# Seven block products in place of eight for the gate and up projections of two pairs of chunks per gated feed-forward

## The chip, the core and the metric

The kernel runs on one core of a Trainium2 chip. TensorE multiplies matrices from SBUF into PSUM, VectorE and ScalarE work on rows and evict PSUM, GpSimd does small things, and SyncE's queue issues the weight loads. The metric is the device time of one execution in microseconds. The kernel before takes 1432.91 us (median of 3 runs, 1431.85 to 1433.77).

## What is computed

The input is one sequence of 256 rows of 1024. A first block (adaptive norm, two kinds of attention, a convolutional feed-forward) is followed by a second block of two layers, each with a gated feed-forward, a mixer, and another gated feed-forward. The change concerns these four feed-forwards:

```python
D_FF = 2816

def swiglu(h, wg, wu, wd):
    return (jax.nn.silu(h @ wg) * (h @ wu)) @ wd

# second_block, for l in (0, 1):
    h = rmsnorm(x, g[0])
    x = x + 0.5 * rmsnorm(swiglu(h, ffn_wg[l, 0], ffn_wu[l, 0], ffn_wd[l, 0]), g[1])
    ...
    h = rmsnorm(x, g[4])
    x = x + 0.5 * rmsnorm(swiglu(h, ffn_wg[l, 1], ffn_wu[l, 1], ffn_wd[l, 1]), g[5])
```

All data are float32.

## The kernel before

**Split products.** Each float32 factor is split into a high part (rounded to the format that TensorE multiplies at full rate, fp32r) and a low part (the rest). A product is three matmuls: high by high, high by low, low by high (line 2552 to 2554). ScalarE writes the high part of a weight tile from the loaded raw tile in two activations of 128x1024 (`split_hi`, line 1936), VectorE the low part in two subtractions (`split_lo`, line 2147).

**Tiles.** A *unit* is a weight tile of 128x2048 floats, 1 MB. Three raw buffers (`RAW`) take the loads in order; SyncE issues a load when the tile three loads earlier has both its parts (line 1756). Three pairs of split buffers (`w_hi`, `w_lo`), and in the stretches of units named by `WIDE` two more (`hi_qk`, `hi_at` and their low ones, in memory that only the attentions use), take the parts. All four gated feed-forwards lie in wide stretches. A tile's split waits until the tile five units before it has been used (`plan.before`, `unit_used`).

**A gated feed-forward.** The columns of the gate and up matrices are cut into 11 chunks (`NFC`) of 256 (`FC`). A chunk has two units, for the input features 0 to 511 and 512 to 1023; each holds, per 128 features, 256 gate columns and 256 up columns. `chunk` (line 2556) runs for each of the 4 feature tiles of a unit and each of the 2 token tiles one split product: stationary the tokens (`hT_hi`, `hT_lo`, 128x128), moving the 512 weight columns, into one PSUM bank per token tile. ScalarE then applies silu to the gate half and VectorE multiplies it with the up half (`upout`, lines 2092 and 2463, one instruction per token tile), TensorE transposes the hidden rows (`hturn`, line 2797), ScalarE and VectorE evict them as `hc_hi` and `hc_lo` (lines 2100 and 2472), and the down projection (one unit, 24 matmuls) adds to four PSUM banks that live through the whole feed-forward.

**Order.** The order is written out by a planner: `build_plan` makes one list of steps, and each engine walks this list and emits its own part of each step, so within an engine's queue the steps stand in this order. `split_ahead(u)` (line 235) puts in, ahead of the product of unit u, the splits of all units up to u + 4 (with five buffers) that are not in yet. `FfnHead.go_on` (line 855) begins a feed-forward: products of chunks 0 and 1 for the second token tile, `upout`, `hturn(0)`, `down(0)`, `hturn(1)`, and then for each chunk from 2 to 9: products of its two units, `upout`, `down` of the chunk before, `hturn`. `tail` does chunk 10 and crosses into the next stage. The lines of `go_on` that matter:

```python
            self.mm(2, 1)
            self.hidden_turn(0)
            pl.split_to(us[3] + 2)
            self.mm(3, 1)
            self.out(1)
            ...
            self.down(0)
            self.hidden_turn(1)
```

`mm(i, t)` is the product of the i-th unit of chunks 0 and 1 with token tile t. `us[3] + 1` is the down unit of chunk 0, `us[3] + 2` the first unit of chunk 2. `down(0)` first calls `split_ahead` for its own unit, so three more units are split in the steps between `out(1)` and `hidden_turn(1)`.

## Time and profile before

| | |
|---|---|
| median of the runs | 1432.91 us |
| profiled execution | 1431.2 us of span |
| TensorE matmul, busy | 1392.6 us (97%), 7039 instructions |
| TensorE weight load, busy | 1157.8 us (81%) |
| VectorE, busy | 926.0 us (65%), 1401 |
| ScalarE, busy | 758.1 us (53%), 1249 |
| weight loads by SyncE | 250.87 MB |
| granted TensorE clock, mean | 0.993 |

Times are from one profiled execution. "Busy" counts instructions that run; matmuls overlap in the pipeline, so their number times their own duration is more than the time they take. A granted clock of 1 is 2.4 GHz, of 0.50 is 1.2 GHz. The four feed-forwards run, roughly, from 440 to 620, 758 to 940, 945 to 1130 and 1248 to 1430 us.

### The profile page before, as it was taken

The numbers are of one execution on the slowest core, as the hardware profiler recorded it, in microseconds if no ns is written. First come the engines' busy times: TensorE is split into PE (matmuls) and PEld (weight loads), VectorE is DVE, ScalarE is ACT, GpSimd is POOL, SyncE is SP. The second block draws the span as 40 slices with busy tenths as digits, with TensorE's granted clock in tenths as the row PEclk, the third lists the DMA queues.
The fourth block names the chain that finished last, engine by engine and source line by source line (L and its number), as shares of the span: only waits on it lengthen the run. The fifth ranks groups of instructions, "written<-read, shape, count | busy, mean of one in ns | idle before, by whom it ended". The sixth has DMA issues, their size and how long they took to land.

```text
span 1431.2 us, 19205 instructions
## 1 busy us (share of the span) xinstructions
PE 1392.6 (97%) x7039; PEld 1157.8 (81%) x7039; DVE 926.0 (65%) x1401; ACT 758.1 (53%) x1249; POOL 79.3 (6%) x133
## 2 busy tenths in 40 slices
PE   4999999999999999999899999999999999999998
PEld 4878877999988888887778888888888877788886
DVE  5677787799777554479986555476545556675453
ACT  4456746755456444366576444465444467574442
POOL 3011100000000000021300000000000100000000
PEclk9999999999999999999999999999999999999999
DMA  9887656477645765544355765547555373565550
GB/s 352 279 293 263 195 173 195 146 268 245 227 146 176 231 196 181 177 133 148 118 173 178 226 199 181 176 134 257 183 185 197 121 210 118 191 230 182 188 165 30
DMA packets 177596, 274.36 MB, mean 192 GB/s; under 512 B 6465, under 2 KB 120897, under 8 KB 177505
## 3 DMA queue, kind: packets, MB, share of 16 engines
q1 hardware_dynamic: 170800, 250.87, 53.2%
q0 software_dynamic: 5552, 20.20, 4.6%
q10 hardware_dynamic: 1153, 2.07, 0.4%
q8 instruction: 58, 0.95, 0.3%
q14 instruction: 33, 0.27, 0.1%
HBM read 272.05 MB, written 1.06 MB: 191 GB/s over the span
## 4 chain that ended last, share of the span: by engine, by line
PE 78%; DVE 4%; issue 1%; ACT 1%; POOL 0%; DVEq 0%; POOLq 0%; ACTq 0%
PE psum L2552 22%; PE psum L2554 22%; PE psum L2553 22%; PE psum L2595 2%; PE psum L2594 2%; PE psum L2592 2%; PE psum L2797 1%; DVE w_lo L2147 1%; PE psum L2649 1%; PE psum L2721 1%; PE psum L2750 0%; DVE attn L2324 0%; PE psum L2664 0%; DVE work L2301 0%; PE psum L2703 0%
## 5 line engine op out<-in xcount | busy, mean ns | idle before, releaser
L2147 DVE TENSOR_TENSOR w_lo<-raw,w_hi 128x1024 fp32r<-128x1024 f32 (+1 forms) x312 | 371.9, 1235 | 115.4 <-ACT w_hi L1936 114.5
L2552 PE MATMUL psum<-w_hi,hT_hi 128*128 128x512 f32 x888 | 357.3, 402 | 6.4 <-DVE hT_lo L2247 3.7
L1936 ACT ACTIVATE w_hi<-raw 128x1024 fp32r<-128x1024 f32 (+1 forms) x312 | 310.8, 1050 | 98.6 <-PE psum L2554 62.2
L2554 PE MATMUL psum<-w_hi,hT_lo 128*128 128x512 f32 x888 | 347.8, 392 | 0.0
L2553 PE MATMUL psum<-w_lo,hT_hi 128*128 128x512 f32 x888 | 347.3, 391 | 0.0
L2552 PEld LDWEIGHTS psum<-w_hi,hT_hi 128*128 128x128 f32 x888 | 167.8, 189 | 45.5 <-issue 10.2
L2554 PEld LDWEIGHTS psum<-w_hi,hT_lo 128*128 128x128 f32 x888 | 167.5, 189 | 36.5
L2553 PEld LDWEIGHTS psum<-w_lo,hT_hi 128*128 128x128 f32 x888 | 168.1, 189 | 32.8 <-issue 0.5
L2147 DVE TENSOR_TENSOR lo_qk<-raw,hi_qk 128x1024 fp32r<-128x1024 f32 (+1 forms) x72 | 84.1, 1209 | 32.5 <-ACT hi_qk L1936 31.8
L2552 PE MATMUL psum<-w_hi,hc_hi 128*128 128x512 f32 x256 | 100.3, 392 | 0.6 <-DVE hc_lo L2472 0.6
L2554 PE MATMUL psum<-w_hi,hc_lo 128*128 128x512 f32 x256 | 99.8, 390 | 0.0
L2553 PE MATMUL psum<-w_lo,hc_hi 128*128 128x512 f32 x256 | 99.7, 389 | 0.0
L2092 ACT ACTIVATE PR<-psum,stat 128x256 f32<-128x256 f32 x88 | 37.6, 472 | 116.0 <-PE psum L2554 114.8
L2147 DVE TENSOR_TENSOR lo_at<-raw,hi_at 128x1024 fp32r<-128x1024 f32 (+1 forms) x72 | 84.2, 1208 | 19.7 <-ACT hi_at L1936 19.4
L2463 DVE SCALAR_TENSOR_TENSOR PR<-psum,stat,PR 128x256 f32<-128x256 f32 x88 | 39.0, 480 | 88.9 <-ACT PR L2092 88.9
L1936 ACT ACTIVATE hi_qk<-raw 128x1024 fp32r<-128x1024 f32 (+1 forms) x72 | 71.4, 1042 | 36.4 <-PE psum L2554 25.1
L2100 ACT ACTIVATE hc_hi<-psum 128x512 fp32r<-128x512 f32 (+1 forms) x48 | 26.9, 561 | 113.1 <-PE psum L2797 113.1
L2472 DVE TENSOR_TENSOR hc_lo<-psum,hc_hi 128x512 fp32r<-128x512 f32 (+1 forms) x48 | 31.0, 646 | 85.1 <-ACT hc_hi L2100 85.1
L1936 ACT ACTIVATE hi_at<-raw 128x1024 fp32r<-128x1024 f32 (+1 forms) x72 | 71.4, 1042 | 25.7 <-PE psum L2554 15.6
L1880 POOL TENSOR_TENSOR stat<-stat,minus_half 128x1 f32<-128x1 f32 (+2 forms) x24 | 17.2, 715 | 1140.8 <-DVE stat L2230 1062.9
L2552 PE MATMUL psum<-hi_qk,hT_hi 128*128 128x512 f32 (+1 forms) x176 | 69.0, 392 | 0.0
L2554 PE MATMUL psum<-hi_qk,hT_lo 128*128 128x512 f32 (+1 forms) x176 | 67.9, 386 | 0.0
(236 smaller groups left out, 2335.5 us busy)
## 6 DMA issues: line engine op xcount, KB each, us to landing
raw<-in_ffn_wg_dram SPq DMA_DIRECT2D x88, 512.0 KB, 4.0
raw<-in_ffn_wu_dram SPq DMA_DIRECT2D x88, 512.0 KB, 5.0
raw<-in_ffn_wd_dram SPq DMA_DIRECT2D x44, 1024.0 KB, 5.0
raw<-in_w_up_dram SPq DMA_DIRECT2D x44, 512.0 KB, 4.9
raw<-in_w_in_dram SPq DMA_DIRECT2D x19, 1024.0 KB, 7.5
ada_raw<-in_w_ada_dram POOLq DMA_DIRECT2D x24, 512.0 KB, 5.1
raw<-in_even_w_in_dram SPq DMA_DIRECT2D x12, 1024.0 KB, 5.1
raw<-in_odd_w_in_dram SPq DMA_DIRECT2D x12, 1024.0 KB, 5.5
```

What stands on the lines that cost most here:

```text
L1936: nc.scalar.activation(hi_of(s)[:, cs], raw_of(s)[:, cs], ACT.Copy).then_inc(ready, 1)
L2092: nc.scalar.activation(sg[:, c_ % 2, t, :], psum[:, use.bank, 0:FC], ACT.Silu, scale=col(a["stat"], "r", t)).then_inc(silu_ready, 1)
L2100: nc.scalar.activation(hidden_of(hc_hi, a["c"], a["ts"]), psum[:, use.bank, 0:2 * w].rearrange("p (f s) -> p f s", f=2), ACT.Copy)\
L2147: nc.vector.tensor_tensor(lo_of(u)[:, cs], raw_of(u)[:, cs], hi_of(u)[:, cs].bitcast(F32), ALU.subtract)\
L2463: nc.vector.scalar_tensor_tensor(hid[:, c_ % 2, t, :], psum[:, use.bank, FC:2 * FC], col(a["stat"], "r", t), sg[:, c_ % 2, t, :], ALU.mult ...
L2472: nc.vector.tensor_tensor(hidden_of(hc_lo, a["c"], a["ts"]), psum[:, use.bank, 0:2 * w].rearrange("p (f s) -> p f s", f=2), hidden_of(hc_h ...
L2552: nc.tensor.matmul(o, a_hi, b_hi, start=start, stop=False)
L2553: nc.tensor.matmul(o, a_hi, b_lo, start=False, stop=False)
L2554: return nc.tensor.matmul(o, a_lo, b_hi, start=False, stop=stop)
L2592: nc.tensor.matmul(o, hi[:, b], hT_hi[:, kk, :], start=kk == 0 and f % 2 == 0, stop=False, skip_group_check=True)
L2594: nc.tensor.matmul(o, hi[:, b], hT_lo[:, kk, :], start=False, stop=False, skip_group_check=True)
L2595: ins = nc.tensor.matmul(o, lo[:, b], hT_hi[:, kk, :], start=False, stop=kk == KT - 1, skip_group_check=True)
```

## The change

In each gated feed-forward the chunks 2, 3 and 6, 7 (`GROUPS`) form two *groups*. For a group, the gate and up projections are one matrix product of 2 x 2 blocks: tokens (2 tiles) by features (2 halves), times features by (512 gate columns | 512 up columns). It is done with seven block products on sums and differences of blocks. Each block product takes one unit of four 128x512 blocks and one token block: 12 matmuls.

- The units of a group are, in order: u1 (gate, lower features, as loaded), u5 = up lower minus gate lower (written to `sums`, the memory of `scr`), u7 = up upper minus up lower (written over the raw tile of u5), u6 = up upper minus `sums` (in place), then the down unit of the chunk before, then u3 (up upper as loaded), u2 (gate upper as loaded) and u4 = gate upper minus `sums`. So there are 7 units to split where there were 4, but still four loads. VectorE forms the four differences (`form`), one unit ahead: `split_lo(s)` begins with `form(s + 1)`. A load waits until the last unit made from the raw tile has its parts (`release`).
- The token blocks are mixed once per feed-forward: step `mixed_rows` (VectorE adds high and low parts of the transposed tokens and makes four sums; ScalarE rounds them to `mixed_hi`) and step `mixed_split` (VectorE writes `mixed_lo`). The products of u5, u7, u6 and u3 read a mixed block, those of u1, u2 and u4 plain ones.
- The products of u1 and u5 are copied out by ScalarE (`gkeep`); VectorE adds up the rest (`gsum`, `gup`, `ggate`), ScalarE applies silu and VectorE multiplies (`ggate`). The rows of both chunks are transposed together per token tile (`gturn`), after the first and the second unit of the chunk that follows, and `down` of both chunks follows there.

The diff, cut to what the argument needs:

```diff
-UNITS = 228
-WIDE = ((25, 99), (113, 183), (195, 228))
+GROUPS = (2, 6)
+MORE = 3 * len(GROUPS)
+UNITS = 228 + 4 * MORE
+WIDE = ((25, 99 + MORE), (113 + MORE, 183 + 3 * MORE), (195 + 3 * MORE, 228 + 4 * MORE))
...
+    def sum_unit(self, load, dst, a, b):
+        u = self.unit(4, BANK, [(0, BANK, load)] if load is not None else [])
+        a, b = (u if v == "own" else v for v in (a, b))
+        self.formed[u] = dict(no=len(self.formed), dst=dst, a=a, b=b, last=self.last_sum if dst == "sums" else None)
+        if dst == "sums":
+            self.last_sum = u
+        return u
...
+            pl.add("mixed_rows", g=self.G[KT - 1, 1])
             self.down(0)
+            pl.add("mixed_split")
             self.hidden_turn(1)
-            for c in range(2, NFC - 1):
+            c = 2
+            while c < NFC - 1:
+                if c in GROUPS:
+                    self.group(c)
+                    c += 2
+                    continue
+                after_group = c - 2 in GROUPS
                 self.up(c, 0)
+                if after_group:
+                    self.group_turn(c - 2, 0)
                 self.up(c, 1)
+                if after_group:
+                    self.group_turn(c - 2, 1)
                 self.out(c)
+                if after_group:
+                    self.down(c - 2)
                 self.down(c - 1)
                 self.hidden_turn(c)
...
+            def product_of(u, use, start, **of):
+                pl.split_ahead(u)
+                pl.add("gprod", unit=u, use=use, start=start, **of)
+            u1 = pl.unit(4, BANK, [(0, BANK, block(gate, 0))])
+            u5 = pl.sum_unit(block(up, 0), "sums", "own", u1)
+            u7 = pl.sum_unit(block(up, 4), u5, "own", u5)
+            u6 = pl.sum_unit(None, "sums", u7, "sums")
+            pl.release[u1], pl.release[u5] = u5, u7
...
+            p1, p5, p7, p6 = (pl.use(b, u) for b, u in zip(banks, (u1, u5, u7, u6)))
+            product_of(u1, p1, True, tile=(0, 0), mixed=None)
+            product_of(u5, p5, True, tile=None, mixed=3)
+            pl.add("gkeep", use=p1, slot=0)
+            product_of(u7, p7, True, tile=None, mixed=2)
+            pl.add("gkeep", use=p5, slot=1)
+            product_of(u6, p6, True, tile=None, mixed=0)
+            pl.add("gsum", kept=(p1, p5), uses=(p6, p7), n=n)
+            self.down(c - 1)
+            u3 = pl.unit(4, BANK, [])
+            pl.raw_from[u3], pl.release[u7] = u7, u3
+            p3 = pl.use(banks[1], u3)
+            product_of(u3, p3, False, tile=None, mixed=1)
+            pl.add("gup", use=p3, n=n)
+            u2 = pl.unit(4, BANK, [(0, BANK, block(gate, 4))])
+            p2 = pl.use(banks[0], u2)
+            product_of(u2, p2, False, tile=(4, 0), mixed=None)
+            pl.add("ggate", t=0, use=p2, stat=self.st, n=n)
+            u4 = pl.sum_unit(None, "sums", u2, "sums")
+            pl.release[u2] = u4
+            p4 = pl.use(banks[2], u4)
+            product_of(u4, p4, False, tile=(4, 1), mixed=None)
+            pl.add("ggate", t=1, use=p4, stat=self.st, n=n)
...
+                        until = plan.release.get(number, number)
+                        sp.wait_ge(hi_ready, until + 1)
+                        sp.wait_ge(lo_ready, until + 1)
...
+                    act.wait_ge(tokens_mixed, 6 * n_mixed[0])
+                    nc.scalar.activation(tokens_hi, tokens, ACT.Copy).then_inc(tokens_hi_ready, 1)
...
+                form(s + 1)
...
+                plus, minus = raw_of(made["a"]), blended if made["b"] == "sums" else raw_of(made["b"])
+                for half in range(2):
+                    cs = half_of(u, half)
+                    nc.vector.tensor_tensor(source_of(u)[:, cs], plus[:, cs], minus[:, cs], ALU.subtract).then_inc(sum_ready, 1)
...
+                    dve.wait_ge(split_done, a["g"] + 1)
+                    for t in range(TT):
+                        ts = slice(t * P, (t + 1) * P)
+                        nc.vector.tensor_tensor(tokens[:, 2 * t:2 * t + 2, :, :].rearrange("p a k n -> p (a k) n"),
+                                                hT_hi[:, :, ts].bitcast(F32), hT_lo[:, :, ts].bitcast(F32), ALU.add)\
+                            .then_inc(tokens_mixed, 1)
+                    n_mixed[0] += 1
+                    base = 6 * n_mixed[0] - 6
+                    x11, x12, x21, x22 = (tokens[:, i, :, :] for i in range(4))
+                    dve.wait_ge(tokens_mixed, base + 2)
+                    nc.vector.tensor_tensor(x22, x21, x22, ALU.add).then_inc(tokens_mixed, 1)
+                    dve.wait_ge(tokens_mixed, base + 3)
+                    nc.vector.tensor_tensor(x21, x11, x21, ALU.subtract).then_inc(tokens_mixed, 1)
+                    dve.wait_ge(tokens_mixed, base + 4)
+                    nc.vector.tensor_tensor(x11, x22, x11, ALU.subtract).then_inc(tokens_mixed, 1)
+                    dve.wait_ge(tokens_mixed, base + 5)
+                    nc.vector.tensor_tensor(x12, x12, x11, ALU.subtract).then_inc(tokens_mixed, 1)
+                elif kind == "mixed_split":
+                    dve.wait_ge(tokens_hi_ready, n_mixed[0])
+                    nc.vector.tensor_tensor(tokens_lo, tokens, tokens_hi.bitcast(F32), ALU.subtract)\
+                        .then_inc(tokens_split, 1)
...
+                elif kind == "gprod":
+                    use, u = a["use"], a["unit"]
+                    wait_free(pe, use)
+                    if a["mixed"] is not None:
+                        pe.wait_ge(tokens_split, n_mixed[0])
+                    for k in range(4):
+                        need_unit(u, k // 2)
+                        if a["mixed"] is not None:
+                            a_hi, a_lo = tokens_hi[:, a["mixed"], k, :], tokens_lo[:, a["mixed"], k, :]
+                        else:
+                            k0, t = a["tile"]
+                            ts = slice(t * P, (t + 1) * P)
+                            a_hi, a_lo = hT_hi[:, k0 + k, ts], hT_lo[:, k0 + k, ts]
+                        o, b = psum[:, use.bank, :], slice(k * BANK, (k + 1) * BANK)
+                        b_hi, b_lo = hi_of(u)[:, b], lo_of(u)[:, b]
+                        nc.tensor.matmul(o, a_hi, b_hi, start=a["start"] and k == 0, stop=False, skip_group_check=True)
+                        nc.tensor.matmul(o, a_hi, b_lo, start=False, stop=False, skip_group_check=True)
+                        ins = nc.tensor.matmul(o, a_lo, b_hi, start=False, stop=k == 3, skip_group_check=True)
+                    ins.then_inc(unit_used, 1)
```

## Rows read from the trace of the kernel before

**Rows 1.** The page, part 1: busy us (share of the span) x instructions.
```profile
PE 1392.6 (97%) x7039; PEld 1157.8 (81%) x7039; DVE 926.0 (65%) x1401; ACT 758.1 (53%) x1249; POOL 79.3 (6%) x133
```

**Rows 2.** The page, part 4: the chain that ended last, by engine and line.
```profile
PE 78%; DVE 4%; issue 1%; ACT 1%; POOL 0%; DVEq 0%; POOLq 0%; ACTq 0%
PE psum L2552 22%; PE psum L2554 22%; PE psum L2553 22%; PE psum L2595 2%; PE psum L2594 2%; PE psum L2592 2%; PE psum L2797 1%; DVE w_lo L2147 1%; PE psum L2649 1%; PE psum L2721 1%; PE psum L2750 0%; DVE attn L2324 0%; PE psum L2664 0%; DVE work L2301 0%; PE psum L2703 0%
```

**Rows 3.** Windows of two feed-forwards: us; busy (x) PE, PEld, DVE, ACT, POOL; clock; DMA.
```profile
778.00:930.00 152.00, 152.00 (x690) 125.79 (x689) 81.07 (x86) 67.39 (x87) 0.54 (x1) 1.00 0.63 203
...
1268.00:1420.00 152.00, 152.00 (x690) 125.74 (x689) 76.51 (x82) 63.37 (x83) 0.50 (x1) 1.00 0.52 168
```

**Rows 4.** Timeline of TensorE, full clock: start, us, engine, line, output<-inputs, count.
```profile
500.11 0.39 PE L2552 MATMUL psum<-w_hi,hT_hi 128*128 128x512 f32 x1
...
500.79 0.39 PE L2552 MATMUL psum<-w_hi,hT_hi 128*128 128x512 f32 x1
```

**Rows 5.** Timeline of VectorE, chunk 1 to 2, first and third feed-forward; [idle before<-releaser].
```profile
453.69 2.35 DVE L2147 TENSOR_TENSOR w_lo<-raw,w_hi 128x1024 fp32r<-128x1024 f32 x2
455.96 0.87 DVE L2463 SCALAR_TENSOR_TENSOR PR<-psum,stat,PR 128x256 f32<-128x256 f32 x2
456.75 2.35 DVE L2147 TENSOR_TENSOR w_lo<-raw,w_hi 128x1024 fp32r<-128x1024 f32 x2
459.46 2.36 DVE L2147 TENSOR_TENSOR w_lo<-raw,w_hi 128x1024 fp32r<-128x1024 f32 x2 [0.36 <-ACT w_hi L1936]
462.81 2.36 DVE L2147 TENSOR_TENSOR lo_at<-raw,hi_at 128x1024 fp32r<-128x1024 f32 x2 [1.00 <-ACT hi_at L1936]
...
958.91 1.23 DVE L2147 TENSOR_TENSOR w_lo<-raw,w_hi 128x1024 fp32r<-128x1024 f32 x1 [0.32 <-ACT w_hi L1936]
```

**Rows 6.** Groups of instructions by form: x count | busy us, mean ns | idle before.
```profile
L2147 DVE TENSOR_TENSOR lo_at<-raw,hi_at 128x1024 fp32r<-128x1024 f32 x70 | 82.7, 1221 | 19.7 <-ACT hi_at L1936 19.4
...
L2451 DVE TENSOR_TENSOR scr<-scr,turned 128x512 f32<-128x512 f32 x4 | 2.6, 688 | 0.0
...
L1936 ACT ACTIVATE hi_qk<-raw 128x1024 fp32r<-128x1024 f32 x70 | 70.1, 1052 | 32.6 <-PE psum L2554 21.3 <-PE psum L2595 3.5 <-DMA raw<-in_w_down_dram 3.3
...
L2100 ACT ACTIVATE hc_hi<-psum 128x512 fp32r<-128x512 f32 x40 | 23.9, 597 | 102.2 <-PE psum L2797 102.2
```

**Rows 7.** The page, part 6: loads, KB each, median us from issue to landing.
```profile
raw<-in_ffn_wd_dram SPq DMA_DIRECT2D x44, 1024.0 KB, 5.0
```

**Rows 8.** Timeline of TensorE: transposes and down projection, first and third feed-forward.
```profile
454.47 0.39 PE L2552 MATMUL psum<-hi_qk,hc_hi 128*128 128x512 f32 x1
...
459.92 0.60 PE L2797 MATMUL psum<-cst,PR 128*128 128x128 f32 x4
...
965.28 0.60 PE L2797 MATMUL psum<-cst,PR 128*128 128x128 f32 x4
```

**Rows 9.** Timeline of SyncE's queue: the load of chunk 2's second unit.
```profile
437.55 0.37 SPq L1764 DMA_DIRECT2D raw<-in_ffn_wg_dram  x1
```

**Rows 10.** Timeline of ScalarE in the first feed-forward: the split of that unit.
```profile
455.05 2.00 ACT L1936 ACTIVATE w_hi<-raw 128x1024 fp32r<-128x1024 f32 x2
```

**Rows 11.** Timeline of TensorE after two idles: [idle before<-releaser].
```profile
28.92 0.76 PE L2552 MATMUL psum<-w_hi,hT_hi 128*128 128x512 f32 x1 [3.49 <-DVE hT_lo L2247]
29.48 0.63 PE L2553 MATMUL psum<-w_lo,hT_hi 128*128 128x512 f32 x1
29.91 0.63 PE L2554 MATMUL psum<-w_hi,hT_lo 128*128 128x512 f32 x1
...
32.04 0.48 PE L2553 MATMUL psum<-w_lo,hT_hi 128*128 128x512 f32 x1
...
701.71 0.87 PE L2721 MATMUL psum<-cst,attn 128*128 128x128 f32 x3 [2.64 <-DVE attn L2341]
```

**Rows 12.** Windows after these idles: us, busy by engine, granted clock before the last two.
```profile
29.00:30.00 1.00, 1.00 (x3) 0.81 (x4) 0.97 (x1) 1.00 (x2) 0.00 (x0) 0.50 1.05 387
...
703.00:704.00 1.00, 1.00 (x8) 0.87 (x6) 0.96 (x6) 0.64 (x2) 0.00 (x0) 0.50 0.00 0
```

More of the change, by code:

```diff
@@ L906, in tail @@
             c = NFC - 1
-            self.up(c, 0)
+            if c - 2 in GROUPS:
+                self.units[c] = self.up_units(c, (0,))
+                self.down_unit(c - 2)
+                self.units[c] += self.up_units(c, (4,))
+                self.open(c)
+                p = self.parts[c][0]
+                pl.split_ahead(p["unit"])
+                product_step("up", p, ks=(0, 1), inc=None)
+                for t in range(TT):
+                    self.group_turn(c - 2, t)
+                product_step("up", p, ks=(2, 3))
+                self.down_part(c - 2)
+            else:
+                self.up(c, 0)
             second = self.parts[c][1]
@@ L1924, in split_hi @@
                     return
-                what = ("w", s)
-                act.wait_ge(weight_loaded[raw_slot[what]], landed[what])
+                made = plan.formed.get(s)
+                if made is None:
+                    what = ("w", plan.raw_from.get(s, s))
+                    act.wait_ge(weight_loaded[raw_slot[what]], landed[what])
                 if plan.before[s] >= 0:
@@ L1935, in split_hi @@
                     cs = half_of(s, half)
-                    nc.scalar.activation(hi_of(s)[:, cs], raw_of(s)[:, cs], ACT.Copy).then_inc(ready, 1)
+                    if made is not None:
+                        act.wait_ge(sum_ready, 2 * made["no"] + half + 1)
+                    nc.scalar.activation(hi_of(s)[:, cs], source_of(s)[:, cs], ACT.Copy).then_inc(ready, 1)
+            n_mixed = [0]
             def turned_mod(a):
@@ L2137, in split_lo, with form @@
                     return
+                form(s + 1)
                 for half in range(2):
                     split_lo_half(s, half)
+            formed = set()
+            def form(u):
+                if u not in plan.formed or u in formed:
+                    return
+                formed.add(u)
+                made = plan.formed[u]
+                for v in (made["a"], made["b"]):
+                    if v != "sums" and v not in plan.formed or v == u:
+                        dve.wait_ge(weight_loaded[raw_slot["w", v]], landed["w", v])
+                if made["dst"] == "sums":
+                    if made["last"] is not None:
+                        dve.wait_ge(hi_ready, made["last"] + 1)
+                        dve.wait_ge(lo_ready, made["last"] + 1)
+                if made["no"]:
+                    dve.wait_ge(sum_ready, 2 * made["no"])
+                plus, minus = raw_of(made["a"]), blended if made["b"] == "sums" else raw_of(made["b"])
+                for half in range(2):
+                    cs = half_of(u, half)
+                    nc.vector.tensor_tensor(source_of(u)[:, cs], plus[:, cs], minus[:, cs], ALU.subtract).then_inc(sum_ready, 1)
             def split_lo_half(u, half):
```

135 lines of the change are left out of this document (125 added, 10 removed).

## Prediction

> **What bounds the kernel now.** I read the page's busy times first: TensorE is busy 97% of the span, VectorE 65%, ScalarE 53% [rows 1]. The chain that ended last is 78% TensorE, two thirds of the span being the three matmul lines of the split product [rows 2]. So what shortens TensorE's stream shortens the kernel, as long as the other engines keep feeding it. Then I read the windows of the four gated feed-forwards: TensorE is busy all 152 us in each of them, VectorE 76.5 to 81.1 (the two ends stand in [rows 3]). On average VectorE has half its time free there. An average does not say where the free time lies, so the last views are the engine timelines of the place where the first group would start [rows 5, 8 to 10].
>
> **What it removes on TensorE.** Two chunks cost 4 weight tiles x 2 token tiles = 8 products of 12 matmuls, 96 in all; a group has 7 products, 84. A 128x512 matmul's own duration reads 0.39 us, but they are pipelined: the starts 500.11 and 500.79 are three pitches apart [rows 4], 0.227 us each, and the pitch is the price. One product is 12 x 0.227 = 2.72 us. Two groups in each of four feed-forwards: 8 x 2.72 = **21.8 us removed**. The transposes (4 per token tile or per chunk, 8 for two chunks either way) and the down projections stay as they are. The loads stay too: four blocks of 1 MB per group before and after, in fewer issues.
> The Trainium skill (TensorE: Matmul & The Clock Gate, "Back-to-back issue gap") gives about 131 ns as the sustained spacing of matmuls of 512 columns. The trace has 227, and the measurement decides; by the page's figure the saving would be 8 x 12 x 0.131 = 12.6 us and the end result 9 us later.
>
> **What it adds on VectorE, per group.** Three more weight tiles to split, each two 128x1024 subtractions of 1.22 us whose pair takes 2.27 us of the queue (453.69 to the next start, 455.96) [rows 5]: 6.8 us. Four block sums (`form`), each again two 128x1024 tensor_tensor on SBUF, the form of [rows 6]: 9.1 us. `gsum`, `gup` and `ggate` are five 128x512 additions and two 128x512 products in place of four 128x256 products (0.79 for a pair, 455.96 to 456.75 [rows 5]): 7 x 0.65 - 1.6 = 3.0 us. About 19 us per group, 38 per feed-forward, and once per feed-forward `mixed_rows` and `mixed_split` (below, 7.6 us): 46 us on top of 79 busy in 152. Averaged, VectorE still fits: 125 of some 150 us. ScalarE gets 3 x 2.0 for the high parts, 1.2 for the two `gkeep` and little else: no bound.
>
> **Does the group itself starve TensorE?** From the first product to the seventh TensorE has 7 x 2.72 + 5.44 (the down projection in between) = 24.5 us of work. VectorE has 8 tiles to split (18.2), 4 sums (9.1) and the evictions (4.6): 31.8 us. It is 7.3 us too slow for the stretch, so it depends on the lead. With five split buffers the tile v is split as soon as v-5 is used, so when a group starts in steady state its four first tiles stand ready. I walked the streams of the second group (chunk 6), with T = 0 its first product: VectorE ends the low part of the down tile at 3.9 (used from 10.9), of u3 at 6.3 (16.3), u2 at 11.1 (19.0), u4 at 13.5 (21.8), of the next chunk's tiles at 18.0 (24.5) and 20.6 (29.9). The smallest margin is 6.5 us; the sum buffer and the three load buffers do not end last in it (each load is issued at least 5 us, its landing time [rows 7], before its tile is wanted). **Second groups cost nothing.** Without that lead each would cost up to 7.3 us.
>
> **The first group is another matter.** Its products need the mixed token blocks, and these are computed late, in program order behind other work. Before: TensorE runs the down projection of chunk 0 from 454.47, transposes chunk 1 at 459.92, and starts chunk 2 right after; call this T0 = 460.3 [rows 8]. VectorE splits chunk 2's first tile at 453.69, i.e. T0 - 6.6, multiplies chunk 1's hidden rows at 455.96, and then splits three more tiles and evicts the transpose [rows 5]. After the change its queue holds, in this order:
> - `form(u5)` 2.3 (its raw tile was issued at 437.55 [rows 9], long landed), low part of u1 2.3, hidden rows of chunk 1 0.8: to 459.1. The transposes at 459.9 are still just in time.
> - `mixed_rows`: two 128x1024 additions 2.3, then four dependent 128x512 ones. 0.69 us each [rows 6] plus a hand-over, 0.75: 3.0. To 464.4.
> - ScalarE must now round the four blocks, one 128x2048 activation. Not in the trace; bounds are 2 x 1.05 (two of [rows 6]) and 1.05 + (1.05 - 0.60) x 2 = 1.95 by the slope between its 128x512 and 128x1024 rows; I take 2.0: to 466.4. It is an in-order wait: the high part of u5, which ScalarE did at 455.05 before, now stands behind it [rows 10]. First half of it at 467.4.
> - VectorE meanwhile does `form(u7)`, then waits for that half: low part of u5 to 469.8, `form(u6)` 472.1, low part of u7 474.4, low part of u6 476.7. These stand ahead of `mixed_split`, because `self.down(0)`, with its `split_ahead`, is planned between `mixed_rows` and `mixed_split`.
> - `mixed_split`, one 128x2048 subtraction. Bounds 2.27 (two of 128x1024 in a row) and 1.22 + 2 x (1.22 - 0.69) = 2.28: to 479.0, hand-over 0.1.
> By the Trainium skill (VectorE: DVE Perf Modes, the section on the TRN2 errata) an fp32 tensor_tensor takes (N + 151) / 0.96 ns, 2.29 us for 2048. No row here has that size; it changes nothing in the sum.
>
> TensorE runs the first product (no mixed block) from 460.3 to 463.0, and then `pe.wait_ge(tokens_split)` holds the second until 479.1: **16.1 us idle**. Behind that wait is everything TensorE has; nobody else is late because of it. After it I followed the streams again: low parts at 481.5 (down tile, used from 487.3), 483.8 (u3), 488.3 (u2, used from 495.4), 490.6 (u4), 495.0 (next chunk, used from 500.9). Margin 5 to 6 us: no second stall. The pattern repeats in all four feed-forwards, with 6.6 us between that split and T0; only in the third is it 6.7 (958.91 and 965.6), with 0.3 us of idle before the split in which part of `form(u5)` fits [rows 5, 8]: 0.5 less there. Sum: 4 x 16.1 - 0.5 = **63.9 us added**. Bounds for one stall: 14 (all hand-overs free, ScalarE's halves earlier) and 18 (0.1 to 0.2 more on each of the dozen dependent steps).
>
> **The clock.** After 3.49 us of idle before 28.92 TensorE restarts at the granted clock 0.50, 1.2 GHz, with matmuls 0.43 us apart, until 32.04, the first one that is shorter again; the idle of 2.64 us before 701.71 did the same (0.50 from 703 to 704) [rows 11, 12]. So I expect each 16 us stall to be followed by some 8 matmuls at half clock: 8 x 0.2 = 1.6 us, 4 x 1.6 = **6.4 us**. Bounds: 0 (the clock stays) and 3.3 us each (twice as long).
> The Trainium skill (TensorE: Matmul & The Clock Gate, "What's actually happening") says that an idle engine falls to the half clock and that activity releases it; both dips agree.
>
> **The sum.** 1431.2 - 21.8 + 63.9 + 6.4 = 1479.7 us of span. The median of the runs is 1432.9, 1.7 over the profiled span: **1481.5 us**.
>
> **Rivals.**
> - *The wait costs less than the product that it saves* (faster). The place is the same wait. It decides at the point where stall and clock together are 5.4 us per feed-forward. If the tokens were ready when the second product wants them, the time would be 1432.9 - 21.8 = 1411. For it: VectorE's half free time [rows 3]. Against: its queue is in order, and [rows 5] shows only 1.4 us of idle between 455.96 and 465, against 19.9 us of work and waits from 459.1 to the end of `mixed_split`. It needs my reading of the order to be wrong. 6%.
> - *Only the token work itself is late*: the splits and sums turn out not to stand in front. From 459.1: 5.3 + 2.0 + 2.3 = 9.7, to 468.8, a stall of 5.8, with the clock 7.4: 4 x 7.4 - 21.8 = +8, 1441. 7%.
> - *VectorE is the bound of every group*: the lead is not there for the second groups (a load buffer held by a sum, or a sum waiting for the single sum buffer). Then 7.3 us more for each of them, 4 x 7.3 = 29: 1511. For it: 31.8 against 24.5. Against: the margins above, and the landing times. 12%.
> - The forecast: 75%.
>
> **Range and chances.** The forecast's own range: stalls of 14 to 18 us (-8, +8) and the clock (-6, +7), 1467 to 1497. Reaching towards the third rival and a little under the forecast: **1460 to 1512**, leaving out about 15%. A measurement of this kernel can tell 0.2%, 3 us, from no change. Faster by more than that: 6%, the first rival. Within it: 2%, a stall that happens to cancel the saving. Slower: 92%.
>
> **What would show it.** In the profile after: 96 matmuls fewer (8 groups x 12); four idles of TensorE of 15 to 17 us, released by a VectorE write of the mixed low blocks, each after the first product of chunk 2; none at chunk 6; the granted clock at 0.50 for about 3 us behind each; VectorE's busy time up by some 180 us, to 1110. If TensorE idles at chunk 6 too, the lead was misjudged; if the four idles are short, the order of VectorE's queue was.

## The result, and the profile after

The changed kernel takes **1484.33 us** (median of 4 runs, 1482.93 to 1485.87); the kernel before, run beside it, 1432.79 (1431.85 to 1433.77). The ratio is **1.0359, 95% interval 1.0345 to 1.0374**: slower by 3.6%. The forecast was 1481.5, range 1460 to 1512.

The profiled execution has a span of 1484.1 us, 52.9 more than before. First the engines' busy times, then the slices of TensorE and of its clock:

```profile
PE 1383.7 (93%) x6943; PEld 1145.2 (77%) x6943; DVE 1101.7 (74%) x1565; ACT 819.8 (55%) x1301; POOL 80.3 (5%) x133
...
PE   5999999999995999999895999987999999959998
...
PEclk8999999999997999999997999997999999989999
```

Against [rows 1] TensorE has 96 matmuls fewer, and its busy share has gone from 97% to 93%. Apart from the first slice, the 13th, 22nd, 28th and 36th of the forty are low in both the engine's row and the clock's, one in each gated feed-forward. The view of waits names them (engine and line, what it waited for: us in total, times, longest):

```profile
PE psum L3046 <- DVE mixed_lo L2380: 62.1, 4, 15.7
```

L3046 is the first matmul of a group's block product, L2380 the subtraction in `mixed_split`. 62.1 us of idle are more than the whole 52.9 by which the span grew. The place in the first feed-forward, TensorE's timeline:

```profile
463.25 0.39 PE L3048 MATMUL psum<-w_hi,hT_lo 128*128 128x512 f32 x1
479.29 0.76 PE L3046 MATMUL psum<-w_hi,mixed_hi 128*128 128x512 f32 x1 [15.66 <-DVE mixed_lo L2380]
```

And VectorE's, from where [rows 5] begin. L2319 is a block sum (`form`), L2327 the low part of a weight tile (L2147 before), L2709 the hidden rows of chunk 1, L2364 to L2377 `mixed_rows`, L2380 `mixed_split`, L2718 the eviction of chunk 1's transposes:

```profile
454.06 2.35 DVE L2319 TENSOR_TENSOR scr<-raw 128x1024 f32<-128x1024 f32 x2
456.33 2.35 DVE L2327 TENSOR_TENSOR w_lo<-raw,w_hi 128x1024 fp32r<-128x1024 f32 x2
458.60 0.87 DVE L2709 SCALAR_TENSOR_TENSOR PR<-psum,stat,PR 128x256 f32<-128x256 f32 x2
459.39 2.35 DVE L2364 TENSOR_TENSOR gate_rows<-hT_hi,hT_lo 128x1024 f32<-128x1024 f32 x2
...
463.95 0.69 DVE L2377 TENSOR_TENSOR gate_rows<-gate_rows 128x512 f32<-128x512 f32 x1
464.56 2.35 DVE L2319 TENSOR_TENSOR raw<-raw 128x1024 f32<-128x1024 f32 x2
467.64 2.36 DVE L2327 TENSOR_TENSOR w_lo<-scr,w_hi 128x1024 fp32r<-128x1024 f32 x2 [0.72 <-ACT w_hi L2065]
470.09 2.36 DVE L2319 TENSOR_TENSOR scr<-raw,scr 128x1024 f32<-128x1024 f32 x2
472.36 2.35 DVE L2327 TENSOR_TENSOR w_lo<-raw,w_hi 128x1024 fp32r<-128x1024 f32 x2
474.63 2.35 DVE L2327 TENSOR_TENSOR lo_at<-scr,hi_at 128x1024 fp32r<-128x1024 f32 x2
476.91 2.28 DVE L2380 TENSOR_TENSOR mixed_lo<-gate_rows,mixed_hi 128x2048 fp32r<-128x2048 f32 x1
479.11 0.68 DVE L2718 TENSOR_TENSOR hc_lo<-psum,hc_hi 128x512 fp32r<-128x512 f32 x1
```

The queue is full from 454.06 to the end of the last line but for one wait of 0.72 us and hand-overs of up to 0.1 us. The mixed tokens were summed by 464.6; their low part starts at 476.9, because two sums and three low parts stand ahead of it. ScalarE's part of the chain, where [rows 10] had the weight tile directly (L2228 is the rounding of the mixed blocks):

```profile
464.68 1.91 ACT L2228 ACTIVATE mixed_hi<-gate_rows 128x2048 fp32r<-128x2048 f32 x1 [9.16 <-DVE gate_rows L2377]
466.50 1.99 ACT L2065 ACTIVATE w_hi<-scr 128x1024 fp32r<-128x1024 f32 x2
```

Two windows (start and end in us, length, then busy us and instructions of PE, PEld, DVE, ACT and POOL, the granted clock, DMA share, GB/s): the time right behind the stall, and the second group:

```profile
479.00:484.00 5.00, 4.71 (x11) 3.77 (x12) 5.00 (x6) 0.60 (x1) 0.00 (x0) 0.50 0.04 15
543.00:575.00 32.00, 32.00 (x146) 26.50 (x145) 28.45 (x29) 21.46 (x25) 0.00 (x0) 1.00 0.68 230
```

Behind the stall TensorE runs at 0.50 of its clock, 1.2 GHz. In the second group it never idles, though VectorE is busy 28.45 of the 32 us.

### The profile page after: what moved, and what is told of

Same layout as the page of the kernel before. It is cut to its first block and busy times, and to the rows that moved or that the text cites. A ratio compares the mean times of both kernels' runs of the same rounds, so it can differ in the third digit from the quotient of the medians.

```text
span 1484.1 us, 19388 instructions
## 1 busy us (share of the span) xinstructions
PE 1383.7 (93%) x6943; PEld 1145.2 (77%) x6943; DVE 1101.7 (74%) x1565; ACT 819.8 (55%) x1301; POOL 80.3 (5%) x133
## 5 line engine op out<-in xcount | busy, mean ns | idle before, releaser
L2327 DVE TENSOR_TENSOR w_lo<-raw,w_hi 128x1024 fp32r<-128x1024 f32 (+1 forms) x312 | 370.8, 1231 | 78.4 <-ACT w_hi L2065 77.5
L2799 PE MATMUL psum<-w_hi,hT_hi 128*128 128x512 f32 x760 | 307.1, 404 | 6.3 <-DVE hT_lo L2493 3.7
L2800 PE MATMUL psum<-w_lo,hT_hi 128*128 128x512 f32 x760 | 298.0, 392 | 0.0
L2801 PE MATMUL psum<-w_hi,hT_lo 128*128 128x512 f32 x760 | 297.9, 392 | 0.0
L2799 PEld LDWEIGHTS psum<-w_hi,hT_hi 128*128 128x128 f32 x760 | 144.2, 190 | 40.5 <-issue 10.0
L2327 DVE TENSOR_TENSOR lo_at<-raw,hi_at 128x1024 fp32r<-128x1024 f32 x74 | 87.4, 1220 | 9.9 <-ACT hi_at L2065 9.7
L2065 ACT ACTIVATE hi_at<-raw 128x1024 fp32r<-128x1024 f32 x74 | 74.1, 1051 | 32.9 <-PE psum L2801 13.9
L2327 DVE TENSOR_TENSOR lo_qk<-raw,hi_qk 128x1024 fp32r<-128x1024 f32 (+1 forms) x70 | 81.7, 1206 | 9.0 <-ACT hi_qk L2065 9.0
L2718 DVE TENSOR_TENSOR hc_lo<-psum,hc_hi 128x512 fp32r<-128x512 f32 (+1 forms) x32 | 19.9, 623 | 52.9 <-ACT hc_hi L2256 52.9
L2799 PEld LDWEIGHTS psum<-w_hi,hc_hi 128*128 128x128 f32 x256 | 48.1, 188 | 13.0 <-DVE hc_lo L2418 1.8
L2801 PEld LDWEIGHTS psum<-w_hi,hc_lo 128*128 128x128 f32 x256 | 48.1, 188 | 10.2
L2095 ACT ACTIVATE hT_hi<-psum,cols 128x128 fp32r<-128x128 f32 x96 | 27.5, 369 | 51.6 <-PE psum L2896 51.6
L2800 PEld LDWEIGHTS psum<-w_lo,hc_hi 128*128 128x128 f32 x256 | 48.1, 188 | 9.2
```

Of the source, the lines that this page charges most:

```text
L2065: nc.scalar.activation(hi_of(s)[:, cs], source_of(s)[:, cs], ACT.Copy).then_inc(ready, 1)
L2095: ins = nc.scalar.activation(tiles_of(hT_hi, k0 + i, 1, a["ts"])[:, 0, :], psum[:, a["use"].bank, i * w:(i + 1) * w], ACT.Copy, scale=g)
L2327: nc.vector.tensor_tensor(lo_of(u)[:, cs], source_of(u)[:, cs], hi_of(u)[:, cs].bitcast(F32), ALU.subtract)\
L2718: nc.vector.tensor_tensor(hidden_of(hc_lo, a["c"], a["ts"]), psum[:, use.bank, 0:2 * w].rearrange("p (f s) -> p f s", f=2), hidden_of(hc_h ...
L2799: nc.tensor.matmul(o, a_hi, b_hi, start=start, stop=False)
L2800: nc.tensor.matmul(o, a_hi, b_lo, start=False, stop=False)
```

## The experiments

The theory: the cost is the four waits for `mixed_split`, made by VectorE's queue order, and the half clock behind them; the seven-for-eight product itself pays. The standing rival: groups of seven cost as much as they save wherever they stand, since VectorE is too slow for them. Each experiment is an edit of the changed kernel, profiled and timed beside the kernel before (1432.6 to 1432.8 each time). Line numbers of the experiments are a few lines off those of the changed kernel, where the edit adds or removes lines. The edits are cut to what matters, with ... for what is left out.

### Only the first group of each feed-forward

```
-GROUPS = (2, 6)
+GROUPS = (2,)
```

> Only chunks 2, 3 form a group; 6, 7 are computed as before the change. If the second group costs nothing but the breaks by its transposes, as its missing idles in the profile after say, each of the four removed ones gives back 2.72 us of matmuls and takes away about 0.35: 1484.3 + 4 x 2.4 = 1493.8 us. Rival (the second group costs VectorE time that TensorE pays somewhere): 1484 us or less.

Measured: 1493.63 us (1492.96 to 1495.61), ratio 1.0427 [1.0411, 1.0443]. The wait stays as it was:

```profile
PE psum L3046 <- DVE mixed_lo L2380: 62.4, 4, 15.9
```

So the four second groups are a gain: without them the kernel is 9.3 us slower, 2.3 us for each. Twelve matmuls of 0.227 us would be 2.7. The traces of the two main kernels show where the rest goes. From the transposes of chunk 5 to those of chunk 8 it is 527.11 to 577.51 before, 50.40 us, and 543.26 to 591.26 after, 48.00: 2.40 less. The missing 0.32 us is one late start, in the changed kernel, of the down projection behind the group's second transposes (TensorE, then its weight loads, then the wait over the whole run, where L2418 is the eviction of these transposes):

```profile
579.59 0.60 PE L3055 MATMUL psum<-cst,PR 128*128 128x128 f32 x4
...
581.17 0.40 PE L2801 MATMUL psum<-w_hi,hc_lo 128*128 128x512 f32 x1
581.60 0.50 PE L2799 MATMUL psum<-w_hi,hc_hi 128*128 128x512 f32 x1
581.94 0.40 PE L2800 MATMUL psum<-w_lo,hc_hi 128*128 128x512 f32 x1
...
581.60 0.19 PEld L2799 LDWEIGHTS psum<-w_hi,hc_hi 128*128 128x128 f32 x1 [0.46 <-DVE hc_lo L2418]
...
PEld psum L2799 <- DVE hc_lo L2418: 3.6, 8, 0.5
```

From 581.17 to 581.60 and on to 581.94 are 0.43 and 0.34 us where the pitch is 0.227: 0.32 lost. The second tile's rows are transposed at 579.59 and wanted seven matmuls later, before their low part is written. It is once per group, 8 in the run: 8 x 0.32 = 2.6 us, a term that the prediction did not have. The standing rival falls for the groups at chunk 6.

### The subtraction twice

```
 elif kind == "mixed_split":
     dve.wait_ge(tokens_hi_ready, n_mixed[0])
+    link(nc.vector.tensor_tensor(tokens_lo, tokens, tokens_hi.bitcast(F32), ALU.subtract))
     nc.vector.tensor_tensor(tokens_lo, tokens, tokens_hi.bitcast(F32), ALU.subtract)\
         .then_inc(tokens_split, 1)
```

> mixed_split is done twice, one after the other, with the same result. Queue theory: each 2.28 us more plus a hand-over on VectorE ahead of tokens_split goes to the end, 4 x 2.35 = 9.4: 1493.7 us, idles of 18.0 us. Rival (the idle ends by something else that came last by chance, such as a load): 1484 us.

Measured: 1493.40 us (1492.25 to 1493.73), ratio 1.0420 [1.0405, 1.0436].

```profile
PE psum L3047 <- DVE mixed_lo L2381: 71.4, 4, 18.0
```

2.28 us more on VectorE come out as 2.3 us more of TensorE's idle, four times. VectorE's queue up to `mixed_split` is the critical path there, with no slack that this shows.

### The subtraction ahead of the down projection's split

```
-            self.down(0)
             pl.add("mixed_split")
+            self.down(0)
```

> mixed_split stands right behind mixed_rows, ahead of the down unit's splits. Queue theory, walked with the durations of the profile after: mixed_split ends at 468.9 in the first feed-forward, but form(u7) and the first half of the low part of u5 now come behind it, so the second product can start at 472.4 and not before: idle 9 us in place of 15.7 and no new idle of more than 1 us: 1484 - 4 x 6.6 = 1458 us. Rival A (only the token work counts): TensorE starts at 469, 1442 us. Rival B (the sum of VectorE's work counts, in any order): 1484 us, with new idles at u7 and u6.

Measured: 1479.77 us (1478.93 to 1481.08), ratio 1.0327 [1.0312, 1.0343]. Expected 1458. TensorE's timeline shows two waits where there was one, and VectorE's what the second is for:

```profile
471.30 0.76 PE L3046 MATMUL psum<-w_hi,mixed_hi 128*128 128x512 f32 x1 [8.84 <-DVE w_lo L2327]
...
479.94 0.79 PE L3046 MATMUL psum<-w_hi,mixed_hi 128*128 128x512 f32 x1 [3.34 <-DVE hc_lo L2718]
...
479.20 0.68 DVE L2718 TENSOR_TENSOR hc_lo<-psum,hc_hi 128x512 fp32r<-128x512 f32 x1
```

The first wait fell from 15.66 to 8.84 us, as forecast (9). But the product of `u7`, the third, goes to the PSUM bank in which chunk 1's transposes still lie, and VectorE evicts those (`hc_lo`) behind the same sums and low parts, at 479.2 in both kernels. This wait of 3.3 to 4.3 us (14.4 in all), and a second fall of the clock in each feed-forward, took most of the gain back: the first waits are 27.3 us shorter in all (62.1 against 34.8), the run only 4.6. The eviction was in my step list as an eviction; that TensorE waits for it was not. It had not mattered in the forecast, because there it follows `mixed_split` directly.

### Groups later in the feed-forward

If the place is at fault, the groups should stand where the tokens are long ready:

```
-GROUPS = (2, 6)
+GROUPS = (4, 8)
```

> The groups are put at chunks 4, 5 and 8, 9 in place of 2, 3 and 6, 7; the token steps stay where they are, right after chunk 1. Queue theory (the stall is there only because the first mixed product comes before VectorE can be through with the splits and the token work): the four idles of 15 to 16 us vanish, the eight products stay saved: 1432.8 - 21.8, plus some 3 us for the more frequent breaks by the group transposes: 1414 to 1417 us. Rival (seven products with 7 units to split make VectorE the bound, wherever the groups stand): the idle moves to chunk 4 with most of its size, 1460 us or more.

Measured: **1436.52 us** (1434.96 to 1441.51), ratio 1.0032 [1.0020, 1.0045]. The wait for the mixed blocks is gone, and 47.8 of the 51.5 us with it. But 1436.5 is some 20 above the 1414 to 1417 expected, and what is left stands at the old place:

```profile
463.96 4.63 DVE L2327 TENSOR_TENSOR w_lo<-raw,w_hi 128x1024 fp32r<-128x1024 f32 x4 [3.00 <-ACT w_hi L2065]
...
470.78 2.28 DVE L2380 TENSOR_TENSOR mixed_lo<-gate_rows,mixed_hi 128x2048 fp32r<-128x2048 f32 x1
472.98 0.68 DVE L2718 TENSOR_TENSOR hc_lo<-psum,hc_hi 128x512 fp32r<-128x512 f32 x1
...
473.81 0.47 PE L2799 MATMUL psum<-w_hi,hc_hi 128*128 128x512 f32 x1 [2.78 <-DVE hc_lo L2718]
```

The first line is VectorE waiting 3.00 us for ScalarE, whose rounding of the mixed blocks stands ahead of a weight tile. The last is TensorE at the down projection of chunk 1, waiting 2.78 us for the eviction that stands behind `mixed_split`. Such waits for `hc_lo` are 12.0 us in 7 places, and 9.5 us of the weight loads' idle are on ScalarE's `w_hi`. The token work, 7.4 us of VectorE (2.35 + 4 x 0.69 + 2.28) and 1.9 of ScalarE per feed-forward, still hurts when nobody waits for its result, by what stands behind it.

### No token mixing

The same two groups as in the change, with `mixed_rows`, `mixed_split` and the waits for them removed; the products read plain blocks of the tokens. This kernel leaves out the mixing, so it does not compute the feed-forward; only its time is of use.

```
-            pl.add("mixed_rows", g=self.G[KT - 1, 1])
             self.down(0)
-            pl.add("mixed_split")
...
-                            a_hi, a_lo = tokens_hi[:, a["mixed"], k, :], tokens_lo[:, a["mixed"], k, :]
+                            m_ = a["mixed"]
+                            ms = slice((m_ // 2) * P, (m_ // 2 + 1) * P)
+                            a_hi, a_lo = hT_hi[:, 4 * (m_ % 2) + k, ms], hT_lo[:, 4 * (m_ % 2) + k, ms]
```

> Left out: mixing and splitting of the token blocks; the products that read mixed blocks read plain ones of the same size. All seven products, the block sums and their splits stay. This shows what is left of the idle when only the weights' work stands in VectorE's queue. By the bank that the run with the earlier split showed: chunk 1's transposes hold bank 6 until VectorE evicts them, now at 471.4, while the third product could start at 466.2: idle 5.3 us and a slow restart of 1.6 to 2: 1432.8 - 21.8 + 2.8 + 4 x 7 = 1442 us. Rival (the token work is the whole stall): 1414 us. Rival (the splits are nearly all of it): over 1465 us.

Measured: 1443.62 us (1441.24 to 1444.01), ratio 1.0072 [1.0058, 1.0086].

```profile
PE psum L3045 <- DVE hc_lo L2715: 20.7, 4, 5.3
```

The token work and the wait for it cost 40.7 of the 51.5 us in that place. The rest is the first group's own sums and splits, which reach TensorE through the same PSUM bank: 5 us each. Even free of the token work, groups at chunk 2 do not pay.

### The idle filled with matmuls

To price the clock alone, TensorE runs 66 matmuls ahead of the wait (66 x 0.227 = 15.0 us), once per feed-forward, into the bank that the waiting product starts anew:

```
+for _ in range(66):
+    nc.tensor.matmul(psum[:, use.bank, :], hT_hi[:, 0, 0:P], hT_hi[:, 0:2, :]..., start=True, stop=True)
 pe.wait_ge(tokens_split, n_mixed[0])
```

> In front of the wait for the mixed blocks TensorE runs 66 matmuls of 128x512 on data that is there already, into the bank that the next product overwrites: 15.0 us of the 15.7 us idle are filled, once per feed-forward. Clock theory: the granted clock stays 1.00, the 41 matmuls that ran at half clock behind the four idles in the profile after (8.7 us more than at full clock) run at full clock: 1484.3 - 8.7 = 1475.6 us. Rival (the slow restart is not due to the idle): 1484 us, clock 0.50 behind the wait.

Measured: **1476.34 us** (1476.07 to 1476.62), ratio 1.0303 [1.0287, 1.0318], 8.0 us less than the changed kernel. The same window as above, and the matmul behind the wait:

```profile
479.00:484.00 5.00, 5.00 (x24) 4.13 (x23) 5.00 (x5) 2.49 (x3) 0.00 (x0) 1.00 0.00 2
...
478.15 0.50 PE L3051 MATMUL psum<-w_hi,mixed_hi 128*128 128x512 f32 x1 [0.66 <-DVE mixed_lo L2380]
```

The clock stays at 1.00 (2.4 GHz) and the same 5 us hold 24 matmuls instead of 11. The wait ends 1.1 us earlier than in the changed kernel (478.15 against 479.29) because this execution reached the place 1.1 us earlier: its transposes of chunk 1 start at 459.19 against 460.29. From there to the end of the wait the path is as long as before, so the half clock behind the four stalls costs these 8 us.

### A place for the token work

What remained was where the token work can stand. I tried three places, with groups at chunks 4 and 8 (4 and 7 in one run), and last a change of the splits' order.

**The subtraction after the output step of chunk 2:**

```
-            pl.add("mixed_split")
...
                 self.out(c)
+                if c == 2:
+                    pl.add("mixed_split")
                 if after_group:
                     self.down(c - 2)
```

> Groups at chunks 4, 5 and 8, 9, and mixed_split moved behind the silu step of chunk 2, so that chunk 1's transposes are evicted ahead of it. If the 20 us that the run with groups 4 and 8 kept are this order (in its profile TensorE waits 2.8 us for hc_lo ahead of down(1), with a slow restart), then those idles shrink to 0.4 us, one of up to 1 us may come ahead of the transposes of chunk 2, and the time falls from 1436.5 to 1416 to 1424 us, faster than the kernel before. Rival (VectorE is short of time as a whole there, and the idle only moves): 1430 us or more.

Measured: 1434.80 us (1431.21 to 1439.50, 11 runs), ratio 1.0013 [1.0003, 1.0023]; a miss by over 10. By its number this is the rival of the expectation, VectorE short of time (1430 or more); the last experiment below decides against it.

```profile
PE psum L3073 <- DVE PR L2710: 9.1, 7, 2.3
...
461.54 1.92 ACT L2229 ACTIVATE mixed_hi<-gate_rows 128x2048 fp32r<-128x2048 f32 x1 [6.88 <-DVE gate_rows L2378]
```

The waits for `hc_lo` shrank from 12.0 to 3.1 us; 9.1 us for the hidden rows (`PR`, the input of the next transposes), most of it at chunk 2, came in their place. ScalarE stood 6.88 us before the rounding, with weight tiles behind it.

**The same, with the second group at chunk 7:** `GROUPS = (4, 7)`.

> As the run before it, but the second group at chunks 7, 8, so that it doesn't run into the last chunk: the idle of 1.0 us ahead of the group transposes in the last chunk goes, 4 us or more. Against it: VectorE has only one chunk (16.8 us, 8.6 of them its own work) between the groups, together 40.4 us of work in 41.3 us of TensorE. If that is too little: idles at chunk 7 of some us each. Expected 1414 to 1422 us by the first, over 1425 us by the second.

Measured: 1443.13 us (1441.04 to 1444.99), ratio 1.0072 [1.0060, 1.0085]. That is 8.3 us more than with the second group at chunk 8. Only chunk 6 stands between the groups now, where it was two chunks, and there TensorE waits once per feed-forward (L2419 is the eviction of a group's transposes). The first of these waits, VectorE's line that it is for, a window behind it, and a window over the second group:

```profile
PE psum L2800 <- DVE hc_lo L2419: 6.1, 4, 2.4
...
536.98 0.60 PE L2800 MATMUL psum<-w_hi,hc_hi 128*128 128x512 f32 x1 [1.77 <-DVE hc_lo L2419]
...
536.24 0.68 DVE L2419 TENSOR_TENSOR hc_lo<-psum,hc_hi 128x512 fp32r<-128x512 f32 x1
...
537.00:540.00 3.00, 3.00 (x8) 2.31 (x9) 3.00 (x5) 0.07 (x1) 0.00 (x0) 0.54 0.82 257
548.00:574.00 26.00, 26.00 (x118) 21.56 (x117) 23.89 (x24) 18.17 (x20) 0.00 (x0) 1.00 0.65 206
```

The wait is not inside the second group, whose 26 us TensorE fills. It stands in chunk 6, at the down projection behind the first group's second transposes: two sums and two low parts for the next group, from 526.55 on, stand ahead of the eviction at 536.24. The move costs 2.1 us per feed-forward, nearly all of the 2.3 us that a second group is worth. It is again awaited work behind work for later; whether another order would cure it, or VectorE's time is too short there, was not tested.

**ScalarE's rounding moved too**, to its own step behind chunk 2's output; the subtraction behind the down projection that follows:

```
-            pl.add("mixed_split")
...
                 self.out(c)
+                if c == 2:
+                    pl.add("mixed_high")
                 if after_group:
                     self.down(c - 2)
                 self.down(c - 1)
+                if c == 2:
+                    pl.add("mixed_split")
...
-                elif kind == "mixed_rows":
+                elif kind == "mixed_high":
                     n_mixed[0] += 1
                     act.wait_ge(tokens_mixed, 6 * n_mixed[0])
```

> Groups at chunks 4, 5 and 8, 9. The sums of the token blocks stay on VectorE right behind chunk 1's silu step, but ScalarE's rounding of them moves behind the silu step of chunk 2, so ScalarE's high parts no longer stand behind it, and mixed_split moves behind down(1)'s splits. In the profile of the run before (groups 4 and 8, late) TensorE waited 1.9 to 2.7 us per feed-forward for chunk 2's hidden rows, because ScalarE stood still for 6.9 us and every load behind it started later. If that is the cause, those 9 us and most of the 3 us for hc_lo go: 1434.8 - 9 to 12 = 1423 to 1426 us. Rival (VectorE is short of time over chunks 2 to 5 as a whole): within 3 us of 1434.8, with the idle in another place.

Measured: 1434.57 us (1429.42 to 1442.57, 12 runs), ratio 1.0019 [1.0005, 1.0032]; a miss by 9, and again within the rival of its expectation (within 3 us of 1434.8, the idle in another place). The waits around chunk 1 are gone, and the profile, of the fastest of the twelve runs, shows a new place, the transposes of chunk 3, right ahead of the group:

```profile
490.06 2.36 DVE L2322 TENSOR_TENSOR scr<-raw,scr 128x1024 f32<-128x1024 f32 x2
492.33 2.35 DVE L2330 TENSOR_TENSOR lo_at<-raw,hi_at 128x1024 fp32r<-128x1024 f32 x2
494.60 0.87 DVE L2712 SCALAR_TENSOR_TENSOR PR<-psum,stat,PR 128x256 f32<-128x256 f32 x2
...
495.62 0.41 PE L3075 MATMUL psum<-cst,PR 128*128 128x128 f32 x2 [2.62 <-DVE PR L2712]
...
496.00:498.00 2.00, 2.00 (x9) 1.59 (x8) 2.00 (x3) 1.71 (x3) 0.00 (x0) 0.58 0.82 252
```

Chunk 3's hidden rows (0.87 us) stand behind the sum for `u6` and a low part, 4.5 us that nobody wants yet. TensorE idles 2.62 us before the transposes of these rows, and its clock falls to 0.58 in the window behind. In the third feed-forward the same wait is 2.72 us, and the clock stays at 1.00 behind it.

**The token sums later as well**, behind `self.hidden_turn(1)`:

```
-            pl.add("mixed_rows", g=self.G[KT - 1, 1])
             self.down(0)
             self.hidden_turn(1)
+            pl.add("mixed_rows", g=self.G[KT - 1, 1])
```

> As the run before it, but VectorE's token sums come behind the eviction of chunk 1's transposes, so the three splits ahead of them, and the loads that these release, are as early as in the kernel before. By the queue theory the best place of the two: 1420 to 1425 us, faster than the kernel before by 0.5 to 0.9%. It loses where chunk 2's hidden rows are then late by the 5.3 us of the sums, less the 2 to 3 us that VectorE is idle there in the kernel before: then about 1430 us, with that idle in the profile.

Measured: 1433.26 us (1429.97 to 1438.65, 12 runs), ratio 1.0002 [0.9992, 1.0012]: a miss by 8, and no change against the kernel before. What is left is mostly the same wait, before the transposes of chunk 3, which is not for the token work:

```profile
PE psum L3075 <- DVE PR L2712: 12.1, 6, 2.8
```

**The hidden rows first.** The step before that one keeps its splits one tile shorter, in `up` of chunk 3 alone; the rest as in the kernel with ScalarE's rounding moved:

```
-            pl.split_ahead(p["unit"])
+            pl.split_ahead(p["unit"], less=1 if (c, i) == (3, 1) else 0)
```

> As the run with spread token steps (early sums), but the split of u7 (with the sum u6 ahead of it) is planned behind the silu step of chunk 3 and not ahead of it. In that run's profile TensorE waited 2.6 us at 495 (1.7 at 813) for chunk 3's hidden rows, which VectorE made 7 us late because form(u6) and the low part of u7 stood ahead of them, and ran 3 us at half clock behind that. If the order is all that is left, these idles go, 9.7 us in all with some 4 to 6 us of slow clock: 1434.6 - 14 = 1419 to 1425 us, faster than the kernel before by 0.5 to 0.9%. Rival (VectorE is full from 480 to 500 whatever its order): the idle moves to the products of u7 or u6, 1431 us or more.

Measured: **1420.76 us** (1414.88 to 1424.88, 6 runs), ratio **0.9914 [0.9897, 0.9932]**: 0.86% faster than the kernel before. The busy row, the wait, the two lines that changed places, and a window over the old idle:

```profile
PE 1374.0 (97%) x6943; PEld 1138.0 (80%) x6943; DVE 1097.1 (77%) x1565; ACT 819.0 (58%) x1301; POOL 80.2 (6%) x133
...
PE psum L3075 <- DVE PR L2712: 2.4, 2, 1.4
...
491.56 0.87 DVE L2712 SCALAR_TENSOR_TENSOR PR<-psum,stat,PR 128x256 f32<-128x256 f32 x2
492.34 2.35 DVE L2322 TENSOR_TENSOR scr<-raw,scr 128x1024 f32<-128x1024 f32 x2
...
480.00:500.00 20.00, 20.00 (x92) 16.54 (x91) 20.00 (x20) 10.65 (x13) 0.00 (x0) 1.00 0.30 97
```

One sum and one low part behind the hidden rows instead of ahead of them are worth 13.8 us by the medians. The two profiled executions are only 9.0 us apart (1427.7 and 1418.7): 7.3 us are these waits (9.7 against 2.4), and the intervals between matmuls at half clock from 440 us on went from 21 to 7, which is 2.7 us. The other 4.8 of the 13.8 us are that the profile without the edit is the fastest of its twelve runs; what the slower ones add was not traced. The seven products do pay, by little, once neither the token work nor a sum stands ahead of what TensorE wants next: the theory holds. What is left of the standing rival is that a group at chunk 2 costs more than it saves, and that with one chunk between two groups the second one's gain is nearly lost.

## Why the prediction was right

The direction and the place came from one step, the walk through VectorE's queue.

- **What bounds the kernel.** Right: TensorE's stream is the time, and each us of its idle at chunk 2 is one of the time; the doubled subtraction showed that (9.3 us more idle, 9.1 us more time).
- **Removed on TensorE, 21.8 us.** Right: 96 matmuls fewer, and a second group is worth 2.3 us net. By an estimate from the 131 ns of the Trainium skill (TensorE: Matmul & The Clock Gate, "Back-to-back issue gap") a group would save 1.6 us at most; that figure does not hold for this stream, whose pitch is 227 ns.
- **Added on VectorE.** Forecast some 180 us, measured 175.7 (926.0 to 1101.7). `mixed_split`, forecast from the slope of [rows 6] at 2.28, took 2.28 us. The Trainium skill (VectorE: DVE Perf Modes, the section on the TRN2 errata) gives 2.29 for it, and now a row agrees. ScalarE's rounding took 1.91, forecast 2.0.
- **Second groups cost nothing.** Right on the wait: no idle in the window 543 to 575. Wrong by 0.32 us a group: "The transposes [...] stay as they are" is true of their number, but the down projection of the second tile now follows so closely that it waits for their eviction.
- **The stall, 16.1 us each, 63.9 in all.** The walk held step by step: low part of `u5` forecast to end at 469.8 and measured at 470.0; `form(u6)` 472.1 and 472.45; low part of `u7` 474.4 and 474.7; of `u6` 476.7 and 477.0; `mixed_split` 479.0 and 479.2. TensorE resumed at 479.29 against 479.1. Since the first product began 0.3 us later too, the stall was 15.8 us beyond the pitch (15.3 in one), 62.7 in all.
- **The clock, 6.4 us.** The mechanism was right, the size was too small. The forecast took 8 slow matmuls from the idle of 3.49 us in [rows 11]; behind the four stalls the trace has 11, 10, 13 and 7 slow intervals, 8.7 us. The filled idle measured it by itself: 8.0.
- **The sum.** -21.8 + 62.7 + 8.7 + 2.6 = 52.2, against 52.9 measured; the forecast had 48.5. The mis-sized clock (+2.3) and the missed waits (+2.6) stand on one side, the stall (-1.2) on the other, so little of the agreement is errors that cancel; 0.7 us were not traced. The growth lies in the four feed-forwards: from the transposes of chunk 1 to the last ones each takes 152.8 us before, and 166.2, 166.1, 166.2 and 165.5 after, 52.7 more together.
- **The rivals.** All three fell. That "only the token work itself is late" is near what the early subtraction was to show, and that run showed a dependency missing in my walk: the PSUM bank of the third product, held by chunk 1's transposes. In the forecast it hides behind `mixed_split`, in the rival it decides: 1441 could not have been reached, for even without any token work the kernel takes 1443.6.

Behind the prediction the expectations that left the order alone came out within 2 us (the second groups, the doubled subtraction, the filled idle, the plain tokens). Of those that moved work, five missed, all the same way, too optimistic by 8 to 22 us (the early subtraction, the later groups, and three places of the token work): I moved the named wait and did not walk the queue at the new place. The run with the second group at chunk 7 had no single figure ahead of it; its worse branch, over 1425, came in. Only the last one, made by reading which VectorE line stood ahead of the awaited one, came out (1419 to 1425 expected, 1420.8 measured).

What stays open: 1420.8 is 7 us above the 1432.8 - 21.8 + 2.6 = 1413.6 that the terms allow. Some 5 us of it are idle in the profile (2.4 on hidden rows, 2.5 on transposes' inputs); the rest was not traced.

## What to carry to other kernels

Fewer products are a gain only if the helper engine's added work stands behind what the bound engine wants next: walk the helper's in-order queue line by line at each place, and ask of each line when its result is wanted, not whether the engine has time on average. A step whose result nobody awaits still delays everything queued behind it, on every engine that takes part, and PSUM banks couple steps that share no data. Moving a wait by reordering needs the same walk again at the new place; here three moves in a row only uncovered the next wait.

## What the runs showed of the hardware

- The length of an idle alone does not tell whether the granted clock falls. With the second group at chunk 7 it fell behind 1.77 us of TensorE's idle (0.54 over 537 to 540, one of the two levels being 0.50); with ScalarE's rounding moved it fell behind 2.62 us (0.58 over 496 to 498) and stayed at 1.00 behind 2.72 us in another feed-forward (the second line is the window behind it):

```profile
999.53 0.63 PE L3075 MATMUL psum<-cst,PR 128*128 128x128 f32 x4 [2.72 <-DVE PR L2712]
...
1000.00:1002.00 2.00, 2.00 (x11) 1.65 (x10) 2.00 (x3) 1.81 (x3) 0.00 (x0) 1.00 0.86 284
```

- Behind idles of 15.1 to 15.7 us the clock came back after 7 to 13 matmuls, behind 3.49 us after some 8 [rows 11]: a longer idle did not clearly cost more.
- Matmuls whose result is thrown away kept the clock up: 66 of them in each idle of 15 us saved 8.0 us of the run.
- Where VectorE runs just in time, the runs scatter more: 1429.4 to 1442.6 in 12 runs with ScalarE's rounding moved, against 1430.6 to 1435.1 in the 23 runs of the kernel before beside it. The profiles don't say why.
